# Feed-forward ends with gate, up, down; small preparing operations laid behind additions

## What is computed

```python
D_FF = -(-8 * D_MODEL // (3 * 256)) * 256

def swiglu(h, w_gate, w_up, w_down):
    return (jax.nn.silu(h @ w_gate) * (h @ w_up)) @ w_down

        h = rmsnorm(x, ffn_pre_g[layer])
        x = x + rmsnorm(swiglu(h, ffn_w_gate[layer], ffn_w_up[layer], ffn_w_down[layer]), ffn_post_g[layer])
```

## Time and profile before

| | us |
|---|---|
| median of 3 runs | 3405.63 |
| lowest and highest | 3403.90, 3414.67 |
| the profiled execution | 3405.91 |
| its span, first to last instruction | 3404.2 |
| PE busy in the span | 3267.7 |
| POOL busy | 2014.3 |
| DVE busy | 1823.2 |
| ACT busy | 819.5 |
| mean granted clock of PE | 0.987 |

### The profile page before, as it was taken

How to read it: one execution, slowest core, us unless ns; L and a number is a source line. 1 busy time by engine, 2 the same in 40 slices (tenths; PEclk the granted TensorE clock), 3 DMA queues, 4 the chain that set the end, 5 groups by cost and what they waited for, 6 DMA issues and landing times.

```text
span 3404.2 us, 40522 instructions
## 1 busy us (share of the span) xinstructions
PE 3267.7 (96%) x15123; PEld 2657.2 (78%) x15123; DVE 1823.2 (54%) x2088; ACT 819.5 (24%) x1183; POOL 2014.3 (59%) x1363
## 2 busy tenths in 40 slices
PE   8999889799999999998999999999999999999998
PEld 5777678688888878886778888877877787877787
DVE  5444424744444457777654344456577666575641
ACT  4333334010111143335200010032112323223211
POOL 4111766788888875456788888876654332414265
PEclk9999989899999999999999999999999999999999
DMA  5110032111111241123112121143224110201143
GB/s 174 33 32 29 19 123 88 38 56 43 55 55 49 62 140 46 43 62 130 38 49 62 49 59 42 53 136 94 79 65 141 43 47 25 71 19 52 37 136 105
DMA packets 242207, 227.94 MB, mean 67 GB/s; under 512 B 8828, under 2 KB 204068, under 8 KB 242104
## 3 DMA queue, kind: packets, MB, share of 16 engines
q1 hardware_dynamic: 221504, 183.46, 18.1%
q10 hardware_dynamic: 20600, 43.07, 3.7%
HBM read 188.65 MB, written 33.64 MB: 65 GB/s over the span
## 4 chain that ended last, share of the span: by engine, by line
PE 77%; DVE 9%; POOL 6%; ACT 3%; issue 3%; ACTq 1%; DMA 0%; DVEq 0%; SPq 0%; POOLq 0%
PE ps L381 24%; PE ps L383 24%; PE ps L382 24%; PE ps L671 1%; POOL Y L789 1%; PE ps L2913 1%; POOL w_lo L371 1%; ACTq L2481 1%; PE ps L1185 1%; ACTq L2509 1%; DVE Y L835 1%; POOL w_hi L369 1%; DVE ml_st_lo L3155 1%; POOL w_lo L1725 0%; ACT b_junk L534 0%
## 5 line engine op out<-in xcount | busy, mean ns | idle before, releaser
L381 PE MATMUL ps<-H_hi,w_hi 128*128 128x512 f32 x2080 | 834.9, 401 | 47.5 <-DVE ffn_sum_up L1626 13.0
L369 POOL TENSOR_TENSOR w_hi<-raw,one_col 128x1024 fp32r<-128x1024 f32 (+1 forms) x151 | 307.3, 2035 | 935.0 <-PE ps L383 920.6
L383 PE MATMUL ps<-H_hi,w_lo 128*128 128x512 f32 x2080 | 814.7, 392 | 0.0
L382 PE MATMUL ps<-H_lo,w_hi 128*128 128x512 f32 x2080 | 813.9, 391 | 0.0
L381 PEld LDWEIGHTS ps<-H_hi,w_hi 128*128 128x128 f32 x2080 | 393.8, 189 | 136.8 <-issue 23.0
L1724 POOL TENSOR_TENSOR w_hi<-raw,one_col 128x512 fp32r<-128x512 f32 x360 | 381.2, 1059 | 181.3 <-PE ps L383 166.4
L1725 POOL TENSOR_TENSOR w_lo<-raw,w_hi 128x512 fp32r<-128x512 f32 x360 | 469.1, 1303 | 28.2
L383 PEld LDWEIGHTS ps<-H_hi,w_lo 128*128 128x128 f32 x2080 | 392.5, 189 | 83.4
L382 PEld LDWEIGHTS ps<-H_lo,w_hi 128*128 128x128 f32 x2080 | 393.5, 189 | 76.8 <-issue 1.9
L371 POOL TENSOR_TENSOR w_lo<-raw,w_hi 128x1024 fp32r<-128x1024 f32 (+1 forms) x151 | 393.0, 2603 | 11.8
L381 PE MATMUL ps<-w_hi,ffn_f_hi 128*128 128x512 f32 x704 | 277.1, 394 | 12.7 <-DVE ffn_f_lo L1584 7.5
(11 more groups left out here) (528 smaller groups left out, 5785.6 us busy)
## 6 DMA issues: line engine op xcount, KB each, us to landing
raw<-in_w_in SPq DMA_DIRECT2D x49, 512.0 KB
raw<-in_ffn_w_gate SPq DMA_DIRECT2D x44, 512.0 KB
raw<-in_ffn_w_up SPq DMA_DIRECT2D x44, 512.0 KB
raw<-in_ffn_w_down SPq DMA_DIRECT2D x44, 512.0 KB
x_dram<-Y SPq DMA_DIRECT2D x32, 512.0 KB, 5.4
b_X<-x_dram SPq DMA_DIRECT2D x24, 512.0 KB, 5.5
raw<-in_ev_w_in SPq DMA_DIRECT2D x17, 512.0 KB
raw<-in_od_w_in SPq DMA_DIRECT2D x16, 512.0 KB
```

Source lines behind the costliest of these rows:

```text
L369: pool.tensor_tensor(w_hi[s][:, :n], raw[s][:, :n], one_col[:, :].broadcast_to([P, n]), ALU.mult).then_inc(split_hi, 1)
L381: pe.matmul(o, l_hi, r_hi, start=first, stop=False, skip_group_check=onto)
L382: pe.matmul(o, l_hi, r_lo, start=False, stop=False, skip_group_check=onto)
L383: return pe.matmul(o, l_lo, r_hi, start=False, stop=last, skip_group_check=onto)
```

## The change

**Ends.** The tenth body (`LAST`) leaves the loop, which now runs eight times, and becomes `ffn{l}_end` with the order gate, up, down. Its up stands at ring places 7 to 13 and its down at 14 to 17. The down uses banks 0 to 3, where the gate was, and waits for the gates to have been taken. The last f goes to tiles of its own, `f_end_hi` and `f_end_lo`, in the space of t1; so the up's first copy and sum go there too, and wait one product longer, until t1 is no more read. The chunks of up are then the third and fourth of the body. `room`, on which the boundary's fetches wait, still is `used` of the body's last product. The tail waits for the last two additions of the down into Y.

**Small operations.** `angles` is cut in two: `decays` (44 operations) for body 0 of layer 0 and `angles` (48) for body 0 of layer 1. `between` now lays two behind every one of the six additions of gate and of up and behind every one of the eight copies into Y, and the rest at the body's end. The two sines go to layer 1, behind ACT's part of body 0. `rotated` (15) goes behind the additions of the last body's down in layer 1, two behind each, with three small tiles of its own.

```diff
     def ffn(l):
         return [(f"ffn{l}_first", 1, gate_up(l, 0, 0)),
                 (f"ffn{l}_one", 1, seven_products(l, 0, 0)),
-                (f"ffn{l}", FF_BLOCKS - 2, seven_products(l, 1, 256)),
+                (f"ffn{l}", FF_BLOCKS - 3, seven_products(l, 1, 256)),
+                (f"ffn{l}_end", 1, down_at_the_end(l, FF_BLOCKS - 2)),
                 (f"ffn{l}_last", 1, down(l, D_FF - 256, 0))]
...
-        GATE, DOWN, UP = 0, 7, 11
+        GATE, DOWN, UP, END_UP, END_DOWN = 0, 7, 11, 7, 14
...
+        f_end_hi, f_end_lo = at("f_end_hi", 32768, [P, 2, S], F32R), at("f_end_lo", 40960, [P, 2, S], F32R)
+        end_sum, end_first = at("end_sum", 40960, [P, HALF]), at("end_first", 43008, [P, HALF])
...
                 if p in (0, 2):
-                    if at == UP:
+                    if f_taken:
+                        e.wait_ge(*f_ready(k, p // 2))
+                    elif at == UP:
                         e.wait_ge(y_added, in_bodies(8, k) + 7 + p // 2)
...
-        def pe_down(e, k, body_0=False):
+        def pe_down(e, k, body_0=False, place=DOWN, bank=4):
             e.wait_ge(*(begun("ready1") if body_0 else f_ready(k, 0)))
+            if bank == 0:
+                e.wait_ge(*gated(k + 1, 0))
...
+                if i < 2 and c == 0:
+                    e.wait_ge(y_added, in_bodies(8, LAST) + 7 + i)
+                ins = token_rows(e, s, 2 * tile_pair(i) + c, i, f_end_hi, f_end_lo)
...
             def first_product(at, bank):
-                e.wait_ge(used, nth(k, at))
-                e.activation(firsts[at][:, :], ps[:, bank, :], ACT.Copy).then_inc(tanh_done, 1)
+                at_end = at == UP and f_out is not None
+                e.wait_ge(used, nth(k, END_UP + 1 if at_end else at))
+                e.activation((end_first if at_end else firsts[at])[:, :], ps[:, bank, :], ACT.Copy).then_inc(tanh_done, 1)
...
             def add(out, bank, other):
                 e.tensor_tensor(out, ps[:, b + bank, :], other[:, :], ALU.add).then_inc(formed, 1)
+                if between:
+                    between(2)
...
         def dve_body(e, k, begins=False, between=None):
-            dve_form(e, k, GATE)
+            dve_form(e, k, GATE, between=between)
+            dve_gates(e, k)
             for _ in dve_down(e, k, begins):
                 if between:
-                    between(5)
-            if between:
-                between(36)
-            dve_form(e, k, UP)
+                    between(2)
+            dve_form(e, k, UP, between=between)
+            dve_fills(e, k)
...
+        def dve_end(e, k):
+            dve_form(e, k, GATE)
+            dve_gates(e, k)
+            dve_form(e, k, UP, END_UP)
+            dve_fills(e, k, END_UP)
+            for t in (1, 0):
+                e.wait_ge(*f_high(k + 1, t))
+                low(e, t, 2 + t, f_end_lo, f_end_hi)
+            rotated = pl["rotated"](e) if l else iter(())
+            for _ in dve_down(e, k, False, END_DOWN, 0):
+                for _ in range(2):
+                    next(rotated, None)
...
-            with e.Fori(0, BODIES - 1) as i:
+            with e.Fori(0, BODIES - 2) as i:
                 load_next(e, loop, i, i + 1)
                 load_rest(e, loop, i, i + 1)
+            load_next(e, end, 0, LAST)
+            load(e, end, 3, 0, made, nth(LAST, GATE + 5))
+            load(e, end, 5, 0, made, nth(LAST, END_UP + 6))
             for c in range(2):
-                load(e, tail, c, 0, made, nth(BODIES - 1, (GATE + 6, DOWN + 3)[c]))
...
+                load(e, tail, c, 0, made, nth(LAST, (GATE + 6, END_UP + 5)[c]))
...
             seven(GATE, 0)
+            if at_end:
+                seven(END_UP, 2)
             for c in range(2):
-                both = raw_chunk(2 + c)
+                both = raw_chunk((4 if at_end else 2) + c)
                 for kk in range(2):
-                    put(DOWN + 2 * c + kk, both[kk])
-            seven(UP, 4)
+                    put((END_DOWN if at_end else DOWN) + 2 * c + kk, both[kk])
+            if not at_end:
+                seven(UP, 4)
...
+            pe_products(e, LAST, GATE, False)
+            pe_products(e, LAST, UP, False, END_UP, True)
+            pe_down(e, LAST, False, END_DOWN, 0)
...
             act_body(e, 0)
-            if l == 0:
+            if l:
                 pl["act"](e)
...
-            angles = pl["angles"](e) if l == 0 else iter(())
+            prepared = pl["angles" if l else "decays"](e)
+            e.wait_ge(*begun("t4_lo"))
...
             dve_body(e, 0, begins=True, between=between)
-            if l:
-                pl["rotated"](e)
-            with e.Fori(0, BODIES - 1) as i:
+            with e.Fori(0, BODIES - 2) as i:
                 dve_body(e, i + 1)
+            dve_end(e, LAST)
```

More of the change, by code:

```diff
@@ L83, in seven_products, with down_at_the_end @@
         return two(A["ffn_w_gate"][l], 256 * (b + 1), step) + down(l, 256 * b, step) + two(A["ffn_w_up"][l], 256 * (b + 1), step)
+    def down_at_the_end(l, b):
+        return two(A["ffn_w_gate"][l], 256 * (b + 1), 0) + two(A["ffn_w_up"][l], 256 * (b + 1), 0) + down(l, 256 * b, 0)
     def ffn(l):
@@ L1425, in ffn @@
         BODIES = FF_BLOCKS - 1
-        first, one, loop, tail = f"ffn{l}_first", f"ffn{l}_one", f"ffn{l}", f"ffn{l}_last"
+        LAST = BODIES - 1
+        first, one, loop, end, tail = f"ffn{l}_first", f"ffn{l}_one", f"ffn{l}", f"ffn{l}_end", f"ffn{l}_last"
         turn = stream.slot(first, 1)
@@ L1515, in pe_down @@
                 if q == 0:
-                    e.wait_ge(made, nth(k, DOWN + 2 * c + 1))
+                    e.wait_ge(made, nth(k, place + 2 * c + 1))
                 if u >= 2:
@@ L1581, in fill, with low @@
             e.scalar_tensor_tensor(pair(target), tha[t][:, :], 0.5, pair(target), ALU.mult, ALU.mult).then_inc(f_dve, 1)
-        def low(e, t, source):
-            e.tensor_tensor(f_lo[:, t, :], pair(source), f32(f_hi[:, t, :]), ALU.subtract).then_inc(f_dve, 1)
+        def low(e, t, source, out=f_lo, hi=f_hi):
+            e.tensor_tensor(out[:, t, :], pair(source), f32(hi[:, t, :]), ALU.subtract).then_inc(f_dve, 1)
         def dve_first(e):
@@ L1620, in dve_first, with dve_form @@
             low(e, 1, 3)
-        def dve_form(e, k, at):
+        def dve_form(e, k, at, place=None, between=None):
             b, total, both = (4 if at == UP else 0), sums[at], firsts[at]
+            if place is None:
+                place = at
+            else:
+                total, both = end_sum, end_first
             def add(out, bank, other):
                 e.tensor_tensor(out, ps[:, b + bank, :], other[:, :], ALU.add).then_inc(formed, 1)
+                if between:
+                    between(2)
             e.wait_ge(*copied(k, at))
-            e.wait_ge(used, nth(k, at + 1))
+            e.wait_ge(used, nth(k, place + 1))
             add(total[:, :], 1, both)
-            e.wait_ge(used, nth(k, at + 2))
+            e.wait_ge(used, nth(k, place + 2))
             e.wait_ge(*sums_made(k, at, 1))
             add(total[:, :], 2, total)
-            e.wait_ge(used, nth(k, at + 3))
+            e.wait_ge(used, nth(k, place + 3))
             add(both[:, :], 3, both)
-            e.wait_ge(used, nth(k, at + 4))
+            e.wait_ge(used, nth(k, place + 4))
             e.wait_ge(*sums_made(k, at, 3))
             add(ps[:, b + 1, :], 1, both)
-            e.wait_ge(used, nth(k, at + 5))
+            e.wait_ge(used, nth(k, place + 5))
             add(ps[:, b + 2, :], 2, both)
@@ L1642, in dve_form, with dve_down @@
             e.wait_ge(*sums_made(k, at, 6))
-        def dve_down(e, k, begins):
+        def dve_down(e, k, begins, place=DOWN, bank=4):
             for u in range(8):
@@ L1657, in dve_down, with dve_gates @@
             e.wait_ge(y_added, in_bodies(8, k) + 8)
-        def dve_body(e, k, begins=False, between=None):
-            dve_form(e, k, GATE)
+        def dve_gates(e, k):
             e.wait_ge(*tanhed(k + 1, 1))
@@ L1761, in pool @@
             o.leave(1)
-            with e.Fori(0, BODIES - 1) as i:
+            with e.Fori(0, BODIES - 2) as i:
                 o.enter(i, 26)
                 pool_halves(e, loop, i, i + 1, False)
-            o.leave(BODIES - 1)
+            o.leave(BODIES - 2)
+            o.enter(0, 26)
+            pool_halves(e, end, 0, LAST, False, True)
+            o.leave(1)
             e.wait_ge(made, nth(BODIES - 1, 17))
@@ L1890, in angles @@
             yield
+        def angles(e):
+            o = dve_steps(e)
+            o(e.tensor_copy(t16, vec("log_dt", 16)))
+            yield
+            yield from exponential(e, o, t16, t16, 16)
             o(e.tensor_tensor(theta[:, 0, :], vec("lam_im", 16), t16, ALU.mult))
@@ new lines, in rotated @@
+            yield
+            o(e.tensor_scalar(turn16[:, :], turn16[:, :], -1.0, None, ALU.add))
+            yield
+            o(e.tensor_tensor(square16[:, :], mag[:, :], rot_im[:, 0, :], ALU.mult))
+            yield
```

(13 more changed lines are left out.)

79 lines of the change are left out of this document (39 added, 40 removed).

## The result

The change is faster by 0.7%, little but clear of noise: 3379.08 us median of five runs (3374.66 to 3385.49) against 3405.63 before, a ratio of 0.9926, 95% interval 0.9915 to 0.9937. In the next comparison, with five more runs of the changed kernel and fifteen of the one before, the medians were 3375.91 and 3405.44 (0.9913, interval 0.9899 to 0.9926). The profiled execution of after took 3374.66 us, 4.4 less than its median.

What follows compares the result with a forecast made beforehand. PE, busy 96%, was taken as the bound, leaving its waits and the lower clock behind them to win. Terms 20.2 - 1.1 + 7.5 = 26.6 us, from 3405.9 to 3379.3; range 3372 to 3390.

Steps and rivals of the forecast that it cites:

- Small operations of layer 0: Layer 0's first body: pairs behind additions and copies fit PE's pace; gain 20.2 us, bounds 14 and 20.6.
- the price of 1.44: First bodies: assumed VectorE time in us for two small operations beside busy POOL, at 0.72 each; bounds 0.4 and 2.3.
- Sines of layer 1: Layer 1's first gate sum of body 1 waits behind eight wide operations and sines; gain -1.1 us, bounds +4 and -5.
- The ends: Last bodies, both layers: gate, up, down removes the gap before the tail; gain 7.5 us, bounds 4.5 and 11.
- the gap of 12.4: Before the tail, both layers: PE's gaps with their slow clock, 12.4 us; only 8.5 expected won at the boundary.
- POOL's 0.6: Last bodies: POOL preparing two sevens in a row delays PE, 0.3 us per layer, bounds 0 and 2.
- the 0.4 for a slow start: Boundary after the tail: 0.4 us deducted for a slow start of PE after the new short wait.
- The signs: Expected trace marks: which PE waits go, stay or appear, including about 5 us on layer 1's gate sum.
- A: Rival: boundary hides its fetch, wide operations are quick; 33.9 us won, 3372 us; chance 0.18.
- B: Rival: pairs stall down of body 0 in both layers, sines later; 15.6 us won, 3390 us; chance 0.15.
- C: Rival: removed wait returns through POOL in end bodies and the boundary, with B; 7 us won, 3399 us; chance 0.05.
- D: Rival: every small operation waits out a whole POOL instruction, everywhere; slower, 3438 us; chance 0.02.

Runs made afterwards that it cites:

- experiment 6: Changed kernel with three small operations instead of two behind each addition and copy of the first bodies, both layers: 3369.34 us, ratio 0.9896; repeated, 3370.66 us.
- experiment 3: Changed kernel with layer 1's eight leftover operations behind the last body's first sums and both sines behind its first up copy: 3370.24 us, ratio 0.99.
- experiment 8: Changed kernel with only layer 1's two sines moved to ScalarE's part of the last body, the eight wide operations left in place: 3374.42 us, single run.
- experiment 9: Changed kernel with six of layer 1's eight wide leftover operations done on 16 elements instead of 160: 3373.14 us, single run.
- experiment 1: Changed kernel with only the new order of the last bodies; small operations and sines placed as before the change: 3397.8 us, ratio 0.9977.
- experiment 7: Changed kernel with four small operations instead of two behind each addition and copy of the first bodies: 3377.14 us, single run.

## Why the prediction was right

The forecast was 3379.3 and 26.6 us; the median came out at 3379.1, the changed stretches of the trace at 28.7. Term by term:

- **Small operations of layer 0**: 20.2 forecast, 20.5 measured. Right in mechanism: pairs fit, and of the 0.4 put on top for runs of slow operations no more than 0.1 came. Beside a busy POOL the 17 pairs took 0.6 to 2.1 us, 1.4 on average, so the price of 1.44 was near. The price was wrong where a third operation was added to it: 2.16 was used for three, and 1.7 was measured (experiment 6).
- **Sines of layer 1**: -1.1 forecast, -2.5 measured. The mechanism held (experiments 3, 8). Mis-sized was "0.78, the 0.72 of the earlier trace rows plus the greater width, 6.3 for eight": they took 8.8 us, seven of eight slow. The average of narrow operations was carried to wide ones, which hardly ever slip in between two POOL instructions (experiment 9). The start, 6.6 behind up's end, was too late by 1.8 and cancelled part of this: the first of the eight began 1690.71 - 1685.95 = 4.8 behind it, since the last two pairs ahead of it took 0.6 and 0.75 and not 1.44.
- **The ends**: 7.5 forecast, 4.7 + 6.0 = 10.7 measured, near the upper bound. The step was right that the gap of 12.4 would not be won whole because the boundary waits for its gain row. The sizes were off, all to the same side: the turning was put 23.4 behind the tail's start and came at 22.7 and 22.4 (the row's copy at 5.8 and 5.5 in place of 6.2, the rest 16.9 in place of 17.2), which is 1.7; the kernel before turned 0.2 us behind its diagonal in each layer, when its tail with the slow matmuls was through (no wait stands there), which makes another 0.5; POOL's 0.6 came to 0.25; and the 0.4 for a slow start came to nothing, since the PE wait ahead of the turning was only 0.5 and the clock stayed at full.
- **The signs.** The waits named did come or stay away as forecast, but two sizes were missed: the wait ahead of the turning was 0.5, not 1 to 2, and the wait on the gate sum 5.9 where about 5 was said.
- **The rivals.** A was right that the ends win nearly all (10.7 of its 11.8), and wrong on the wide operations. B, C and D need additions into Y that fall behind, and at two behind each there were none; C also needs POOL to hold PE in the last bodies, where PE lost 0.25 us in layer 1 and nothing in layer 0. D is half right: a slow operation does wait for the end of a POOL instruction. But not each does: 9 of the 15 in the earlier trace rows were slow (the "two in three" of the prediction is three in five), and three behind each fit.

The forecast of 587 for layer 1's stretch was 588.1, and 580 for layer 0's was 579.5. That the median fell on the forecast to 0.3 us is luck twice over. The terms missed by +0.3, -1.4 and +3.2, which partly cancel. And the 28.7 of the trace became 26.6 in the medians of one comparison and 29.5 in those of the next.

## What to carry to other kernels

Lay small serial work behind operations that wait for the matmul engine anyway, count how many fit in one period, and test one more and one fewer: here two and three behind each cost PE almost nothing (under 0.4 us a layer), four cost 6.0 and 7.5. Count what is left over at the end as well: in layer 1 it cost 8.7 us, more than the 6.2 that it replaced. When a gap is filled by work moved up, look at the fetches that start at its old beginning: the gap was their cover, and here 12.4 us of gap gave 10.7. A producer with a table load behind it (here two sines) belongs where its engine has time to spare, even a whole phase later.

## What the runs showed of the hardware

A VectorE operation on 8 to 24 elements beside a busy GpSimd takes 0.16 to 0.20 us, or else 0.3 to 1.3 and then ends with a GpSimd instruction (86 of 86 within 0.04 us). An addition or copy out of PSUM keeps its time there (0.69 for 128x512, 1.22 for 128x1024, with or without GpSimd). Behind such an operation the short ones came a little cheaper than in a row: three in 1.7 us on average against 2.2; the eight wide ones in a row took 1.1 us each.

The length of a PE wait did not alone decide what followed. Behind waits up to 1.5 us in these stretches the matmuls kept full pace, 0.23 us apart. Between 1.9 and 3.7 us both were seen: a wait of 1.9 was followed by slow matmuls (0.43 apart) in the kernel before and by full pace in experiment 1, waits of 2.5 and 3.54 by slow matmuls in experiment 7, waits of 3.2 and 3.53 by full pace in experiments 8 and 9, 3.7 by slow matmuls each time. Waits of 4.5, 5.9 and 13.0 were always followed by the lower clock, granted 0.50, with 5 to 13 slow matmuls behind them, 1.4 to 2.9 us. So a priced stall carries an uncertainty of 1 to 3 us for the clock alone.
